# Summing the third modulation row on VectorE instead of TensorE in a one-layer hybrid block

## What is computed

```python
mod = (jax.nn.silu(c) @ w_mod[i] + b_mod[i])[:, None, :]
sh1, sc1, g1, sh2, sc2, g2 = jnp.split(mod, 6, axis=-1)
h = modulate(rms_norm(x, mix_norm_pre[i]), sh1, sc1)
p = h @ w_in[i]
...
x = x + g1 * rms_norm(mix @ w_out[i], mix_norm_post[i])
hf = modulate(rms_norm(x, ffn_norm_pre[i]), sh2, sc2)
x = x + g2 * rms_norm(swiglu(hf, w_gate[i], w_up[i], w_down[i]), ffn_norm_post[i])
```

## Time and profile before

| | us |
|---|---|
| median of 3 runs | 1610.84 (1610.16 to 1612.67) |
| the profiled execution | 1613.92 |
| its span, first to last instruction | 1612.2 |
| PE busy in it | 1538.3 (95%) |
| DVE busy in it | 1033.4 (64%) |
| ACT busy in it | 739.2 (46%) |
| POOL busy in it | 222.2 (14%) |

### The profile page before, as it was taken

One profiled execution on the slowest core, in us unless ns is written; L12 is line 12 of the kernel. 1 busy time (PEld: TensorE's weight loads), 2 busy tenths in 40 slices (PEclk: granted clock), 3 DMA queues, 4 the chain that ended last, 5 costly groups with the idle time before them and its releaser, 6 DMA issues.

```text
span 1612.2 us, 25110 instructions
## 1 busy us (share of the span) xinstructions
PE 1538.3 (95%) x9297; PEld 1295.0 (80%) x9297; DVE 1033.4 (64%) x1435; ACT 739.2 (46%) x1042; POOL 222.2 (14%) x236
## 2 busy tenths in 40 slices
PE   3888999999999999999999999999999999999998
PEld 0557888898889888898877888888888888888786
DVE  1446899999997766665577544545454454777554
ACT  5535534443345745455357444444444443443332
POOL 2000223333242324244100000000000000000000
PEclk9998999999999999999999999999999999999999
DMA  9994566555655556564373766666666666998653
GB/s 351 382 397 116 167 199 196 190 190 183 208 179 176 171 171 209 170 196 132 118 261 117 212 194 186 192 185 192 184 193 192 187 190 191 339 321 319 222 187 136
DMA packets 190977, 334.58 MB, mean 208 GB/s; under 512 B 14706, under 2 KB 80354, under 8 KB 189985
## 3 DMA queue, kind: packets, MB, share of 16 engines
q1 hardware_dynamic: 190194, 330.89, 63.3%
q0 software_dynamic: 688, 2.39, 0.5%
HBM read 331.15 MB, written 2.10 MB: 207 GB/s over the span
## 4 chain that ended last, share of the span: by engine, by line
PE 82%; DVE 9%; DMA 2%; ACT 2%; SPq 2%; issue 2%; DVEq 0%; ACTq 0%
PE PS L1886 67%; DVE cacc L1752 3%; DMA first<-in_w_mod_dram 2%; DVE w_lo L1465 2%; PE PS L2107 2%; PE PS L2155 2%; PE PS L1892 2%; PE PS L2201 2%; SPq L756 2%; DVE sil L1586 1%; PE PS L2053 1%; PE PS L2097 1%; PE PS L1982 1%; DVE xyi L1645 1%; ACT L973 1%
## 5 line engine op out<-in xcount | busy, mean ns | idle before, releaser
L977 ACT ACTIVATE w_hi<-raw 128x1024 fp32r<-128x1024 f32 (+1 forms) x422 | 443.2, 1056 | 494.8 <-PE PS L1886 418.1
L1432 DVE TENSOR_TENSOR w_lo<-raw,w_hi 128x1024 fp32r<-128x1024 f32 x264 | 323.0, 1225 | 309.9 <-ACT w_hi L977 309.8
L1886 PE MATMUL PS<-w_hi,h_hi 128*128 128x512 f32 x704 | 275.2, 391 | 0.0
L1886 PE MATMUL PS<-w_hi,h_lo 128*128 128x512 f32 x704 | 274.3, 390 | 0.0
L1886 PE MATMUL PS<-w_lo,h_hi 128*128 128x512 f32 x704 | 274.1, 389 | 0.0
L1886 PE MATMUL PS<-h_hi,w_hi 128*128 128x256 f32 (+1 forms) x784 | 237.6, 303 | 0.0
L1465 DVE TENSOR_TENSOR w_lo<-raw,w_hi 128x1024 fp32r<-128x1024 f32 (+1 forms) x158 | 195.8, 1250 | 56.5 <-ACT w_hi L977 56.5
L1886 PE MATMUL PS<-h_hi,w_lo 128*128 128x256 f32 (+1 forms) x784 | 221.5, 283 | 0.0
L1886 PE MATMUL PS<-h_lo,w_hi 128*128 128x256 f32 (+1 forms) x784 | 221.4, 282 | 0.0
L1886 PEld LDWEIGHTS PS<-h_hi,w_hi 128*128 128x128 f32 (+1 forms) x784 | 148.3, 189 | 36.1 <-issue 32.0
L1886 PEld LDWEIGHTS PS<-w_hi,h_lo 128*128 128x128 f32 x704 | 132.3, 188 | 27.6
(11 more groups left out here) (323 smaller groups left out, 2338.4 us busy)
## 6 DMA issues: line engine op xcount, KB each, us to landing
raw<-in_w_in_dram SPq DMA_DIRECT2D x128, 512.0 KB, 3.8
raw<-in_w_mod_dram SPq DMA_DIRECT2D x96, 512.0 KB, 5.3
raw<-in_w_gate_dram SPq DMA_DIRECT2D x88, 512.0 KB, 3.6
raw<-in_w_up_dram SPq DMA_DIRECT2D x88, 512.0 KB, 3.6
raw<-in_w_down_dram SPq DMA_DIRECT2D x88, 512.0 KB, 4.6
first<-in_w_mod_dram SPq DMA_DIRECT2D x64, 512.0 KB, 9.3
raw<-in_w_out_dram SPq DMA_DIRECT2D x32, 512.0 KB, 4.3
gin<-in_w_mod_dram SPq DMA_DIRECT2D x32, 512.0 KB, 6.0
```

Of the source, the lines that this page charges most:

```text
L977: act.activation(out_ap, in_ap, ACT.Copy).then_inc(S[kind], 1)
L1432: dve.tensor_tensor(w_lo[:, slot, :], raw[:, (R0 + n) % RING, :], w_hi[:, slot, :].bitcast(F32), ALU.subtract).then_inc(S["lo"], 1)
L1886: ins = pe.matmul(out_ap, a[i], b[j], start=start and n == 0, stop=stop and n == 2, skip_group_check=grouped)
```

## The change

The third group is taken out of `mr`, and out of `gates`, which spreads the 32 steps left over the first two thirds of the stream, the same steps at the same slots as before. The third row is now summed by VectorE. The row of 2048 is cut into four quarters q, and each quarter takes eight steps `md(q, j)`. A step uses one ring slot of 512 KB, which holds two rows of w_mod for each partition, [128 x 2 x 512], and two VectorE instructions of 128x512: mrw = raw \* csil + mrw. So partition p sums its own 16 rows, and the second instruction waits for the first. After eight steps TensorE sums over the partitions: `mcol(2, q)` multiplies each 128-column piece of `mrw` as stationary operand by a column of ones, four fp32 matmuls with one column, which also turns the row. VectorE then adds the bias to four columns of `modc` (`mcc(2, q)`).

The steps start 5 slots after the convolution and the second row are done and come every 7 slots (`AFTER["md0"]`, `AFTER["md"]`): 21 of them while the input projection runs, the rest beside the output projection. The last steps stand one by one before the units (0,3), (1,3), (2,4) and (2,5), and `s2` follows `mcc(2, 3)`. `mcol(1)` now follows `mrc(1)` at once. The load of `x` has a step of its own, `xin`, at its old place. The pairs of steps that made an inverse root (a logarithm and an exponential on ScalarE, which stood side by side) are one step each, with the same instructions and a semaphore of ScalarE's own between them. The distances in `AFTER` are set anew; most steps keep their slot, some of `kk`, `dec`, `vn`, `on`, `oT`, `taps` and `csilu` move by one to four slots.

```diff
@@ -87,17 +87,17 @@
 
 QS = 4
...
-         "gates": 15, "conv": 4, "rush": 1, "vb1": [0, 2, 1, 1, 3, 2, 0, 5]}
+         9], "gates": 15, "conv": 4, "rush": 1, "md": 7, "md0": 5, "vb1": [0, 2, 2, 2, 3, 3, 0, 5]}
...
@@ -209,7 +209,9 @@
 
 def make_plan():
     plan = [("masks", ()), ("zero", ()), ("csil", ())]
-    mr = [(grp, j) for grp in range(MR) for j in range(KT)]
+    mr = [(grp, j) for grp in range(MR - 1) for j in range(KT)]
+    rows = [x for q in range(NQ) for x in [[("md", (q, j))] for j in range(KT // 2)] + [
+        [("mcol", (MR - 1, q)), ("mcc", (MR - 1, q))]]]
 
     placed = {}
 
@@ -234,6 +236,7 @@
     soon = []
     late = []
     slot = [0, 0, 0]
+    row_slot = [None]
 
     def advance():
 
@@ -257,6 +260,11 @@
         advance()
         if soon and slot[0] >= soon[0][0]:
             follow(soon.pop(0)[1])
+        if row_slot[0] is None and ("dw", (NP - 1, NDW - 1)) in placed and ("mcc", (MR - 2,)) in plan:
+            row_slot[0] = slot[0] + AFTER["md0"]
+        if rows and row_slot[0] is not None and slot[0] >= row_slot[0]:
+            put(rows.pop(0))
+            row_slot[0] += AFTER["md"]
         if late and (slot[0] % AFTER["conv"] == 2 or AFTER["rush"] * len(late) > slot[2] - slot[0]):
             put(late.pop(0))
 
@@ -275,6 +283,8 @@
             plan.append(("mrm", (grp, j)))
             if j == KT - 1:
                 plan.append(("mrc", (grp,)))
+                if grp == MR - 2:
+                    plan.extend([("mcol", (grp,)), ("mcc", (grp,))])
         del mr[:n]
 
...
     for n, cu in enumerate(STREAM):
         if cu == ("z", LAT, NP - 1):
             gates(len(mr))
-            plan.extend([("mcol", (MR - 1,)), ("mcc", (MR - 1,))])
...
-            gates(MR * KT * done // total - (MR * KT - len(mr)))
+            gates((MR - 1) * KT * 3 * done // (2 * total) - ((MR - 1) * KT - len(mr)))
...
     until(("mix_lo", (NP - 1,)))
     assert not any(queue for _, queue in queues)
-    plan.append(("s2", ()))
+    while len(rows) > KT // 2 + 1:
+        put(rows.pop(0))
+    if not rows:
+        plan.append(("s2", ()))
+    plan.append(("xin", ()))
     for n, (c, kg) in enumerate(WO_REST):
         if n < 2:
             plan.extend([("gdiag", (0, 2 * n)), ("gdiag", (0, 2 * n + 1))])
         u = ("wo", c, kg)
+        if rows:
+            put(rows.pop(0))
+            if not rows:
+                plan.append(("s2", ()))
         if c == 3:
             plan.extend([("hi", (u,)), ("lo", (u,))] + [("mm", (u, half * NT)) for half in range(2)])
             if kg == 5:
+            if u[0] == "md":
+                _, q, j = u
+                col = (1 + MR) * D + 512 * q
+                return w_mod_v[:, 2 * j:2 * j + 2, col:col + 512]
...
-                elif kind in ("hi", "mrm"):
-                    for u in [key[0]] if kind == "hi" else [("mr", *key, 0), ("mr", *key, 1)]:
+                elif kind in ("hi", "mrm", "md"):
+                    for u in [key[0]] if kind == "hi" else [("md", *key)] if kind == "md" else [("mr", *key, 0), ("mr", *key, 1)]:
...
                             old = RINGED[n - RING]
                             if old[0] == "mr":
                                 need(sp, "mrm", *old[1:3])
+                            elif old[0] == "md":
+                                need(sp, "md", *old[1:])
                             else:
                                 need(sp, "hi", old)
...
@@ -976,9 +999,14 @@
             def copy(out_ap, in_ap, kind):
                 act.activation(out_ap, in_ap, ACT.Copy).then_inc(S[kind], 1)
 
-            def inverse_root(out_ap, log_ap):
+            def inverse_root(out_ap, log_ap, in_ap, eps, scale):
 
                 using(EXP_LN)
+                n_chain[0] += 1
+                act.activation(log_ap, in_ap, ACT.Ln, bias=eps, scale=scale).then_inc(ch_act, 1)
+                act.wait_ge(ch_act, n_chain[0])
                 return act.activation(out_ap, log_ap, ACT.Exp, scale=-0.5)
 
...
                 elif kind == "s2":
-                    need(dve, "mcc", 2)
+                    need(dve, "mcc", MR - 1, NQ - 1)
...
+                elif kind == "md":
+                    q, j = key
+                    n = at_ring["md", q, j]
+                    dve.wait_ge(landed[n % RING], 16 * (n // RING + 1))
+                    if j == 0:
+                        need(dve, "mcol", *((MR - 1, q - 1) if q else (MR - 2,)))
+                    for i in range(2):
+                        part, col = raw[:, n % RING, 512 * i:512 * (i + 1)], csil[:, LAT, 2 * j + i:2 * j + i + 1]
+                        if j or i:
+                            ins = dve.scalar_tensor_tensor(out=mrw[:, :], in0=part, scalar=col, in1=mrw[:, :],
+                                                           op0=ALU.mult, op1=ALU.add)
+                        else:
+                            ins = dve.tensor_scalar(mrw[:, :], part, col, None, ALU.mult)
+                        if i == 0:
+                            step(ins)
+                    ins.then_inc(done, 1)
+                    if j < KT // 2 - 1:
+                        need(dve, "md", q, j)
+                elif kind == "mcc" and key[0] == MR - 1:
+                    grp, q = key
+                    need(dve, "mcol", *key)
+                    at = KT * grp + 4 * q
+                    dve.tensor_tensor(modc[:, at:at + 4], PS[:, BANK["mcol", key], 0:4],
+                                      vcol[:, VC_MR + at:VC_MR + at + 4], ALU.add).then_inc(done, 1)
...
-                                need(pe, "mrc", MR - 1)
+                                need(pe, "mrc", MR - 2)
...
+                elif kind == "mcol" and key[0] == MR - 1:
+                    grp, q = key
+                    need(pe, "md", q, KT // 2 - 1)
+                    b = aux(pe, kind, key)
+                    for n in range(4):
+                        ins = pe.matmul(PS[:, b, n:n + 1], mrw[:, P * n:P * (n + 1)], ones[:, 0:1], start=True, stop=True)
                     ins.then_inc(done, 1)
```

More of the change, by code:

```diff
@@ L350, in make_plan @@
         unit(("wo", c, kg), QS, beside)
-    assert not late and not soon
+    assert not late and not soon and not mr
     until(("mix_lo", (NP - 1,)))
     assert not any(queue for _, queue in queues)
-    plan.append(("s2", ()))
+    while len(rows) > KT // 2 + 1:
[3 more added lines that the diff above has]
+    plan.append(("xin", ()))
     for n, (c, kg) in enumerate(WO_REST):
@@ L476, in layer @@
     SQUARED = {name: [step for step in PLAN if step[0] == name] for name in ("ysq", "psq")}
-    UNITS = [u for u in RINGED if u[0] != "mr"]
+    UNITS = [u for u in RINGED if u[0] not in ("mr", "md")]
     at_unit = {u: n for n, u in enumerate(UNITS)}
@@ L611, in sem @@
             return es.enter_context(nc.semaphore(name))
-        S = {kind: sem(f"s_{kind}") for kind in TOTALS if kind not in ("fh", "fl", "ft")}
+        S = {kind: sem(f"s_{kind}") for kind in TOTALS if kind not in ("fh", "fl", "ft", "xin")}
         S["fh"], S["fl"] = S["hi"], S["lo"]
@@ L1060, in _ @@
                 elif kind == "orc":
-                    need(act, "ort", *key)
-                    inverse_root(rstd[:, 16:20], rtmp[:, 16:20]).then_inc(S[kind], 1)
+                    need(act, "osq", *key)
+                    inverse_root(rstd[:, 16:20], rtmp[:, 16:20], sums[:, 16:20], cst[:, 0:1], 1.0 / P).then_inc(S[kind], 1)
                 elif kind == "lnr":
-                    need(act, "lsd")
-                    inverse_root(cx[:, 0, :], cx[:, 1, :]).then_inc(S[kind], 1)
+                    need(act, "lva", 3)
@@ L1066, in _ @@
+                    inverse_root(cx[:, 0, :], cx[:, 1, :], cx[:, 0, :], cst[:, 0:1], 1.0 / DC).then_inc(S[kind], 1)
                 elif kind == "yrc":
                     t, = key
-                    need(act, "yrt", t)
-                    inverse_root(rstd[:, 6 + t:7 + t], rtmp[:, 6 + t:7 + t]).then_inc(S[kind], 1)
+                    need(act, "ysm", t)
+                    inverse_root(rstd[:, 6 + t:7 + t], rtmp[:, 6 + t:7 + t], sums[:, 6 + t:7 + t], cst[:, 0:1],
+                                 1.0 / D).then_inc(S[kind], 1)
@@ L1248, in _ @@
                     copy(rb[:, :, :].rearrange("p a b -> p (a b)"), PS[:, BANK["o", key], :], kind)
-                elif kind == "ort":
-                    need(act, "osq", *key)
-                    using(EXP_LN)
-                    act.activation(rtmp[:, 16:20], sums[:, 16:20], ACT.Ln, bias=cst[:, 0:1],
-                                   scale=1.0 / P).then_inc(S[kind], 1)
                 elif kind == "mix_hi":
```

87 lines of the change are left out of this document (31 added, 56 removed), and 10 rows, old and new, of the table AFTER.

## The result

The changed kernel takes 1617.59 us (median of 16 runs, 1612.76 to 1619.91) against 1611.14 us for the kernel before (16 runs, 1609.92 to 1613.52). The ratio is 1.0034, with a 95% interval of 1.0026 to 1.0042: 5.5 us slower (4.2 to 6.8); the two medians differ by 6.45. The forecast was 1598 us with a range of 1592 to 1608. The time came out at rival D's 1617.7, which is in part luck: D's terms are not the measured ones, as the last part shows.

The account below looks back on a forecast made before the run. TensorE, busy 95% of the span, was taken as the bound. Terms -18.7 - 1.6 + 3.6 + 1 + 2.5 = -13.2 us from the median 1610.84 gave 1598 us, range 1592 to 1608.

Parts of the forecast that it names:

- rival D: Middle: pairs ahead of gh or pi delay TensorE 0.75 us each, 15.7 in all; kernel slower, 1617.7 us; chance 0.08.
- Removed from TensorE, 18.7 + 1.6 us: TensorE: 16 third-row steps at 1.17 us go, 18.7 off; moving the turning of rows takes 1.6 us more off.
- The rule of the first paragraph: 545 to 850 us: a microsecond off TensorE is one off the kernel, unless the engine taking the work makes TensorE wait.
- The wait at 542 us absorbs the copy's: Second row's turning: 1.18 us of copy wait and transposes fit into TensorE's 2.24 us wait for VectorE's pi.
- rival A: Everything hides: VectorE's idle time swallows all sums, the ring keeps up, the clock stays high; 1592.4 us; chance 0.13.
- Added on TensorE, 3.6 us: Four column sums mcol(2, q) on TensorE, eight passes each, 0.9 us apiece, 3.6 us added.
- Added on VectorE in the middle, +1 us: Beside the input projection: 21 pairs, 31.3 us into 99.9 us of VectorE idle time, cost 1 us (0 to 5).
- The length of a sum, 745 ns: Each of VectorE's 64 sums of 128x512 takes 745 ns, 47.7 us in all (41 to 79).
- The end, +2.5 us: Beside the output projection: 11 pairs and added ring loads beside x cost 2.5 us (0.5 to 7.9).
- rival B: End of the mixer chokes: pairs at 806 to 824 us and loads beside x cost 7.9 us; 1603 us; chance 0.20.
- The 4.5 us that I had for VectorE falling behind there: 806 to 824.5 us: six pairs, 8.9 us, meet 4.4 us of idle pieces, so VectorE falls some 4.5 us behind.
- At nothing: Later s2, merged inverse roots, equal weight bytes and moved table distances priced at 0, the distances with 2 us either way.

Follow-up runs that it names:

- two_rows: The kernel before with the third row not computed (its 16 sums, 32 loads, copy and transposes left out): 1599.36 us, 11.6 off.
- two_rows_light: The kernel before without the third row, and convolution taps of the last three latent pairs cut to 8 of 256 columns: 1594.61 us.
- no_row: The changed kernel without the third row's 32 loads, each VectorE sum 8 columns of a constant tile: 1601.78 us.
- mid_small: The changed kernel with the first 21 pairs of sums, beside the input projection, 8 columns wide instead of 512: 1608.18 us.
- xin_late: The changed kernel with the 2 MB load of x waiting for the last sum step md(3,7): 1611.99 us.
- end_small: The changed kernel with the last 11 pairs of sums, beside the output projection, 8 columns wide instead of 512: 1613.78 us.
- before_new_table: The kernel before with the new table of distances, nothing else changed: 1611.49 us.

## Why the prediction was wrong

In the order of its terms:

- **Removed from TensorE, 18.7 + 1.6 us: too large, 11.6 measured (two_rows).** The step that failed is taking the gap of 1.17 us between two weight loads as what TensorE's end moves by. TensorE's busy time did fall nearly as forecast, by 17.3 us in the traces, or 1.05 for a step, but 3.5 us of it became idle time, since VectorE's results were then waited for, and with VectorE relieved the removal is worth 3.7 more (two_rows_light). Some 3 us between the traces and the medians stay open. The rule of the first paragraph, a microsecond off TensorE is one off the kernel unless the other engine makes it wait, had its exception already at work in the kernel before: the earlier trace rows was one of those waits.
- **The wait at 542 us absorbs the copy's: right**, 2.24 to 0.62. The clock stayed up there (500 to 545 us 1.00 instead of 0.97), as rival A had it, but it fell elsewhere.
- **Added on TensorE, 3.6 us: right as a pace** (0.90 us from 619.47 to 620.37 for eight passes). As a cost of the kernel it is not confirmed: no_row and two_rows, each against its own kernel before, differ by 1.5 us (resampled, -1.4 to 3.5), with the moved turning and the merged inverse roots in it.
- **Added on VectorE in the middle, +1 us: the other large error.** mid_small gives 9.4, outside my own bound of 5. The failing sentence is "in proportion 31.3 more make 0.9". Idle time of an engine that works in turn with the bound is no store that any work can be put into: VectorE waits for TensorE at `gh` and is itself waited for a few microseconds later, in order. No single wait holds it: against mid_small TensorE waits 1.3 us more for `sil`, 1.2 for `zi`, 1.1 for `eq` and 0.8 for `at`, and no more for `pi`. Up to the last `hc_lo` its idle time is 12.8 us against 7.3 in mid_small, and the clock adds an estimated 3.2 (0.94 over 545 to 600 us and 0.97 over 650 to 700, where mid_small has 0.97 and 1.00: 0.03 x 55 + 0.03 x 50), 8.7 of the 9.6 by which the traces differ; the clock's share was not tried by itself. The Trainium skill (TensorE: Matmul & The Clock Gate, Part 1) has the clock fall after low activity, and the rows at 821 us agree: 0.55 behind a wait of 5.16 us. I had weighed the clock only for the wait that shrinks, not for those that grow.
- **The length of a sum, 745 ns: 837.** The longest is the 1.75 us beside `mkl`. The Trainium skill (GPSIMD Engine Reference, section 1, Specifications) has GpSimd contend with VectorE instructions of two SBUF inputs, and the trace agrees: 1.75 us there, 735 ns at the shortest. Against the 745 all sums take 64 x 0.09 = 6 us more of VectorE's time, an estimated 1.6 us of the kernel at 0.45 us for a pair of 1.67, which does not decide the sign.
- **The end, +2.5 us: low.** Its length grew by 6.7 us, and rival B's mechanism was there: `x` and the ring's loads together (5.6 us, xin_late), with the clock at 0.55 behind it. The failing sentence is that the late loads are `x`'s as often as a unit's: one unit's load took 10.26 us, and ScalarE's order put the gate copies behind it. The 4.5 us that I had for VectorE falling behind there did not show: with its sums narrow the end is 0.9 shorter (end_small).
- **At nothing: right** for the table, which is neutral for the old work (before_new_table). The merged inverse roots were not tried by themselves.

On one scale: 1611.0 - 11.6 (removal) + 1.5 (column sums and the moved turning) + 3.4 (loads) + 12.4 (sums) = 1616.7, against 1617.6. The sum closes by construction, since its terms are differences along one row of kernels; it tests nothing. Rival D named the mechanism and asked 0.58 us for each middle pair to come out slower by more than 3.2 us; 0.45 was enough because the removal gave 8.7 us less than I had booked. That its 1617.7 meets the measured time is luck: its 20.3 for the removal and 15.7 for the middle were too large by 8.7 and 6.3 us, which cancel in part. It deserved more than 0.08: I had taken the number of VectorE's waits for TensorE as evidence against it, and they say only that the chain goes to and fro.

## What to carry to other kernels

When work moves from the bound to an engine that hands it results, don't fill that engine's idle share: look at what is queued behind each inserted instruction and who waits for that, and price the removal with the waits that then come forward. A run with the removed work simply left out gives the ceiling of such a change first; here it was 11.6 us for a change whose work elsewhere costs more. Look also at what stands behind a wait for a load in its engine's order: here copies that needed no load waited with it. A large load that is not urgent should wait for a stretch in which the ring is not tight.
